# A two-block transformer on one core: the order of the first weight chunks, conv norm in pieces, pooling over band columns, residual and output in halves

## The reference, cut to what matters

```python
# block 1
mod = silu(c) @ w_ada + b_ada                      # six rows of 1024: shift, scale, gate, twice
h = rms_norm(x, norm1_w) * (1 + sc1) + sh1
proj = h @ w_in                                    # 2840 columns: q, six k/v, gates, b_gate, c_gate, u
...                                                # compressed, selected and window attention
y_conv = b_gate * short_conv(c_gate * u, conv_w)   # width 3
mix = rms_norm(concat([o_attn, y_conv]).reshape(.., 16, 64), out_norm_w)
x = x + g1 * (mix @ w_out)
x = x + g2 * hier_moe(rms_norm(x) * (1 + sc2) + sh2)      # top 2 of 64 experts
# block 2, layer l = 0, 1
h = h + g1 * (even_mixer(xn, xcn) if l == 0 else pool_mix(xn, pool_w) * pool_scale)
h = h + g2 * ((silu(hn @ w1) * (hn @ w3)) @ w2)           # 2816 hidden columns
return rms_norm(h, final_g)
```

## Time and profile before

| | before |
|---|---|
| median of three runs | 1738.36 us |
| the profiled execution | 1738.92 us, span 1737.1 us |
| TensorE matmul busy | 1390.4 us, 80% of the span |
| TensorE weight load busy | 868.6 us, 50% |
| VectorE busy | 653.3 us, 38% |
| ScalarE busy | 161.8 us, 9% |
| moved by DMA | 590.09 MB, mean 340 GB/s |
| mean granted TensorE clock | 0.901 |

### The profile page before, as it was taken

One profiled execution on the slowest core, in us unless ns is written; L12 is line 12 of the kernel. 1 busy time (PEld: TensorE's weight loads), 2 busy tenths in 40 slices (PEclk: granted clock), 3 DMA queues, 4 the chain that ended last, 5 costly groups with the idle time before them and its releaser, 6 DMA issues.

```text
span 1737.1 us, 24743 instructions
## 1 busy us (share of the span) xinstructions
PE 1390.4 (80%) x10724; PEld 868.6 (50%) x10725; DVE 653.3 (38%) x1096; ACT 161.8 (9%) x409; POOL 5.0 (0%) x10
## 2 busy tenths in 40 slices
PE   6798998766667666676667666778999999999997
PEld 4787854322212221222122112216877999989997
DVE  2367553501100110011001010107446777768775
ACT  2003320000000000000000000002422000120001
POOL 1000000000000000000000000000000000000000
PEclk9999999888888887878888898879999999999999
DMA  9989959999999999999999999996944554424541
GB/s 402 363 337 402 421 209 397 400 431 431 431 432 431 432 430 432 431 432 431 431 432 430 432 431 431 431 430 271 400 171 154 206 210 175 187 81 158 210 181 61
DMA packets 46555, 590.09 MB, mean 340 GB/s; under 512 B 5360, under 2 KB 7824, under 8 KB 9376
## 3 DMA queue, kind: packets, MB, share of 16 engines
q1 hardware_dynamic: 42896, 583.89, 80.9%
q10 hardware_dynamic: 3600, 5.34, 0.9%
HBM read 586.58 MB, written 2.62 MB: 339 GB/s over the span
## 4 chain that ended last, share of the span: by engine, by line
DMA 48%; PE 43%; DVE 6%; ACT 2%; issue 1%; SPq 0%; DVEq 0%; ACTq 0%
DMA ring<-in_w 45%; PE ps L2042 5%; PE ps L2037 4%; PE ps L2038 4%; PE ps L1551 3%; PE ps L1841 3%; PE ps L1729 3%; PE ps L1862 3%; PE ps L1488 3%; PE ps L2053 2%; PE ps L2055 2%; PE ps L2056 2%; DMA ring<-in_w_in 2%; DMA ring<-in_w_ada 1%; DVE ring_parts L819 1%; PE ps L1955 1%
## 5 line engine op out<-in xcount | busy, mean ns | idle before, releaser
L1841 PE MATMUL ps<-ring,mixT 128*32 128x512 f32 x2016 | 300.6, 732 | 161.0 <-DMA ring<-in_w 160.1
L1862 PE MATMUL ps<-ring,arena 128*32 128x512 f32 x1024 | 170.5, 799 | 112.7 <-DMA ring<-in_w 101.5
L1841 PEld LDWEIGHTS ps<-ring,mixT 128*32 128x32 f32 x2016 | 61.9, 121 | 375.1 <-issue 195.2
L1194 DVE TENSOR_TENSOR arena<-arena,ps 128x512 f32<-128x512 f32 x16 | 11.0, 689 | 488.5 <-PE ps L1841 488.5
L819 DVE TENSOR_TENSOR ring_parts<-ring,ring_parts 128x1024 fp32r<-128x1024 f32 (+3 forms) x119 | 189.7, 1625 | 1.1
L2037 PE MATMUL ps<-mixT_parts,ring_parts 128*128 128x256 f32 x704 | 169.5, 281 | 0.6 <-issue 0.6
L2038 PE MATMUL ps<-mixT_parts,ring_parts 128*128 128x256 f32 x704 | 169.4, 281 | 0.0
L1862 PEld LDWEIGHTS ps<-ring,arena 128*32 128x32 f32 x1024 | 32.7, 128 | 231.2 <-DMA ring<-in_w 150.4
L816 DVE CAST ring_parts<-ring 128x1024 fp32r<-128x1024 f32 (+3 forms) x119 | 100.4, 891 | 113.5 <-DMA ring<-in_f 72.4
L2037 PEld LDWEIGHTS ps<-mixT_parts,ring_parts 128*128 128x128 f32 x704 | 133.2, 189 | 2.1 <-issue 1.4
L2038 PEld LDWEIGHTS ps<-mixT_parts,ring_parts 128*128 128x128 f32 x704 | 132.8, 189 | 0.8
(11 more groups left out here) (379 smaller groups left out, 1421.9 us busy)
## 6 DMA issues: line engine op xcount, KB each, us to landing
ring<-in_w SPq DMA_DIRECT2D x190, 2048.0 KB, 25.8
ring<-in_ada_w SPq DMA_DIRECT2D x24, 2048.0 KB, 12.4
ring<-in_f SPq DMA_DIRECT2D x22, 2048.0 KB, 7.7
ring<-in_w_ada SPq DMA_DIRECT2D x12, 2048.0 KB, 16.4
ring<-in_f SPq DMA_DIRECT2D x22, 1024.0 KB, 5.3
ring<-in_w_in SPq DMA_DIRECT2D x5, 2048.0 KB, 22.8
ring<-in_w_out SPq DMA_DIRECT2D x2, 2048.0 KB, 11.4
ring<-in_mix_in SPq DMA_DIRECT2D x2, 2048.0 KB, 21.9
```

The lines of the kernel that those rows point to most:

```text
L1841: last = mm(ps[rows[u], j, :], XeT[:, 2 * m + k, rows[u]], w[:, u, k * FE:(k + 1) * FE], start=(m == 0 and k == 0), stop=(m == 3 and k == 1))
L1862: last = mm(ps[rows[u], m, :], heT[:, k, rows[u]], w[:, u, m * 512:(m + 1) * 512], start=(k == 0), stop=(k == FE // P - 1))
```

## The change

Seven edits, in the order of the program:

1. The numbers of the chunks. The two compression chunks, W4, W5 and W2 come earlier, and each pair of the condition chunks 6 to 11 (in the order of `w_ada`) goes behind the piece that it preceded.
2. W1 is loaded between the second and the third condition chunk, and split before the first condition round; its product takes the low part of the weights before the low part of `h`. TensorE still consumes the chunks in the order of their numbers.
3. VectorE's condition round 1 comes after the split of W5.
4. The conv's norm: ScalarE multiplies the conv result by the norm weight, four ACTIVATE of 128x256, between the square roots for q and the first `queries`; VectorE takes the reciprocal in three pieces inside attention, and one product of 128x1024 replaces the four of L992.
5. In the last step of each SwiGLU, TensorE puts the group (f = 0, t = 1, m = 1) behind (f = 1, t = 1, m = 0), and signals when t = 1, m = 0 is complete. The last two steps are written out instead of looped. `residual_ffn` takes t = 1 in two halves of 512 columns.
6. Pooling: token tile 0 gives columns 0 to 135 of the output, tile 1 columns 120 to 255, instead of all 256 each.
7. The final norm and the store run in halves of 512 columns.

```diff
--- before.py
+++ after.py
@@ -44,6 +44,7 @@
...
 CHUNK = 4096
+POOL = (2, 4, 8, 16)
 ARENA = 11264
@@ -73,9 +74,9 @@
...
 
-RA = (0, 1, 2, 3, 6, 7, 10, 11, 16, 17, 20, 21)
-RW = (24, 4, 22, 8, 14, 18)
-RC = 12
+RA = (0, 1, 2, 3, 6, 7, 14, 15, 18, 19, 22, 23)
+RW = (24, 4, 20, 8, 12, 16)
+RC = 10
 RL0 = 26
@@ -388,7 +389,7 @@
...
             front.update({RC: (A["cmp_k_w1"], CHUNK), RC + 1: (A["cmp_v_w1"], CHUNK)})
-            for n in sorted(front):
+            for n in (0, 1, RW[1], 2, 3, *sorted(n for n in front if n > RW[1])):
                 load(n, *front[n])
@@ -477,10 +478,10 @@
...
                         ffn_step(l, c, i)
-            for t in range(NT):
-                sp.wait_ge(x_new, 6 * NT + t + 1)
-                sp.dma_start(out[0, t * P:(t + 1) * P, :], xn[:, t, :]).then_inc(out_done, 16)
-            sp.wait_ge(out_done, 16 * NT)
+            for n, (t, a) in enumerate(((0, 0), (0, 512), (1, 0), (1, 512))):
+                sp.wait_ge(x_new, 6 * NT + n + 1)
+                sp.dma_start(out[0, t * P:(t + 1) * P, a:a + 512], xn[:, t, a:a + 512]).then_inc(out_done, 16)
+            sp.wait_ge(out_done, 16 * 4)
 
@@ -586,6 +587,9 @@
...
 
+            for f in range(4):
+                last = nc.scalar.activation(mixT[:, 4 + f, :], cT[:, f, :], ACT.Copy, scale=V("outn")[:, 4 + f:5 + f])
+            last.then_inc(cv_sd, 1)
             q5 = q.rearrange("p t (h i d) -> p t h i d", h=2, d=HD)
@@ -874,6 +878,7 @@
...
             norm(0)
+            split_w(RW[1], 512)
             dve.wait_ge(bias_in, 16)
@@ -881,9 +886,7 @@
...
             high_h(1, 2)
-            high_w(RW[1], 512)
             low_h(1)
-            low_w(RW[1], 512)
             split_w(RW[3], 512)
@@ -916,7 +919,6 @@
...
             split_w(RW[4], 512)
-            ada_round(1, 6)
             dve.wait_ge(tab_in, 32 + 16 * NH)
@@ -924,6 +926,7 @@
...
             split_w(RW[5], 512)
+            ada_round(1, 6)
 
@@ -970,9 +973,6 @@
...
             last.then_inc(k_n, 1)
-            dve.wait_ge(cv_sd, 1)
-            link(nc.vector.reciprocal(sq, sq))
-
             qs = xnf[:, 1024:1536].rearrange("p (h d) -> p h d", d=HD)
@@ -987,13 +987,12 @@
...
             ts(kTw, ps[:, 2, 256:512], kn[:, 2:3], None, ALU.mult).then_inc(k_ready, 1)
-            done(dve, RW[0])
-            for f in range(4):
-                last = stt(mixT[:, 4 + f, :], cT[:, f, :], V("outn")[:, 4 + f:5 + f], sq[:, f * T:(f + 1) * T], ALU.mult,
-                           ALU.mult)
-            last.then_inc(cv_mix, 1)
-            dve.wait_ge(cv_mix, 1)
+            dve.wait_ge(cv_sd, 2)
             link(nc.vector.memset(L[:, 0:2, C1 + NC:C0], 0.0))
+
+            def conv_norm(a, b):
+
+                return nc.vector.reciprocal(sq[:, a * T:b * T], sq[:, a * T:b * T])
 
@@ -1005,6 +1004,10 @@
...
                 ts(qT, ps[:, 1, 256:512], V("qn"), SCALE, ALU.mult, ALU.mult).then_inc(a_qT, 1)
+                if u == 0:
+                    conv_norm(0, 1)
+                elif u == 1:
+                    link(conv_norm(2, 4))
                 tb = tab4[:, :, u, :]
@@ -1051,8 +1054,10 @@
...
             logits(0)
+            conv_norm(1, 2)
             probabilities(0)
             logits(1)
+            tt(mixT[:, 4:8, :], mixT[:, 4:8, :], sq.rearrange("p (f t) -> p f t", f=4), ALU.mult).then_inc(cv_mix, 1)
             combined(0)
@@ -1276,6 +1281,19 @@
...
 
+            def residual_ffn(l):
+
+                dve.wait_ge(g_ev, 4 + 2 * l)
+                yy = ps[:, 4:8, :].rearrange("p (t c) n -> p t (c n)", t=NT)
+                out0, out1 = NT * (NF * (l + 1) - 1) + 1, NT * NF * (l + 1)
+                for t, cols, ready in ((0, slice(0, D), (f_out, out0)), (1, slice(0, 512), (y_first, 3 + l)),
+                                       (1, slice(512, D), (f_out, out1))):
+                    dve.wait_ge(*ready)
+                    link(tt(xn[:, t, cols], yy[:, t, cols], gB[:, cols], ALU.mult))
+                    last = tt(x[:, t, cols], x[:, t, cols], xn[:, t, cols], ALU.add)
+                    if cols.stop == D:
+                        last.then_inc(x_new, 1)
+
             def residual(b0, n, ready):
@@ -1446,7 +1464,7 @@
...
             modulation(modcol[:, 2, :], V("nmix1"))
-            residual(4, 4, lambda t: dve.wait_ge(f_out, NT * (NF - 1) + t + 1))
+            residual_ffn(0)
 
@@ -1462,13 +1480,15 @@
...
             ffn(1)
-            residual(4, 6, lambda t: dve.wait_ge(f_out, NT * (2 * NF - 1) + t + 1))
+            residual_ffn(1)
 
...
                 link(nc.vector.reciprocal(rstd[:, t:t + 1], sd2[:, t:t + 1]))
-                stt(xn[:, t, :], x[:, t, :], rstd[:, t:t + 1], rowB, ALU.mult, ALU.mult).then_inc(x_new, 1)
+                for cols in (slice(0, 512), slice(512, D)):
+                    stt(xn[:, t, cols], x[:, t, cols], rstd[:, t:t + 1], rowB[:, cols], ALU.mult, ALU.mult
+                        ).then_inc(x_new, 1)
 
@@ -1540,10 +1560,9 @@
...
 
-            def product(o, h, w, h_first, split):
-
-
-                for n, (a, b) in enumerate(((0, 0), (1, 0), (0, 1))):
+            def product(o, h, w, h_first, split, w_low_first=False):
+
+                for n, (a, b) in enumerate(((0, 0), (0, 1), (1, 0)) if w_low_first else ((0, 0), (1, 0), (0, 1))):
                     if split and n:
@@ -1578,18 +1597,17 @@
...
                                    (lambda k: hh[:, k, :], lambda k: hl[:, k, :]),
-                                   (lambda k: wH[:, k, c], lambda k: wL[:, k, c]), False, split if f == 0 else None)
+                                   (lambda k: wH[:, k, c], lambda k: wL[:, k, c]), False, split if f == 0 else None,
+                                   w_low_first)
                 return last
...
             pe.wait_ge(h_split, 1)
-            features(RW[1], 512, 2, 2, low_parts(1, 1))
+            features(RW[1], 512, 2, 2, low_parts(1, 1)[::-1], True)
             tokens(RW[1], 512, 256, [ps[:, 3, t * 256:(t + 1) * 256] for t in range(NT)], None).then_inc(ring_used, 2)
...
             features(RW[3], 512, 4, 0, low_parts(1, 2)).then_inc(ring_used, 2)
-            ada_chunk(RA[6], 6, 2, 0)
-            ada_chunk(RA[7], 6, 3, 0)
             pe.wait_ge(blk_ready, 1)
@@ -1606,9 +1624,8 @@
...
             last.then_inc(hidT_tr, 1)
-            pe.wait_ge(ada_ev, 2)
-            ada_chunk(RA[8], 6, 0, 0)
-            ada_chunk(RA[9], 6, 1, 0)
+            ada_chunk(RA[6], 6, 2, 0)
+            ada_chunk(RA[7], 6, 3, 0)
             pe.wait_ge(hidT_ev, 1)
@@ -1623,10 +1640,13 @@
...
             tr(ps[:, 7, 256:256 + NC], kcn[0:NC, :], ident[0:NC, 0:NC]).then_inc(kc_tr, 1)
+            pe.wait_ge(ada_ev, 2)
+            ada_chunk(RA[8], 6, 0, 0)
+            ada_chunk(RA[9], 6, 1, 0)
+            pe.wait_ge(win_dve, 1)
+            tokens(RW[2], 280, 0, [ps[:, 2 + t, 0:280] for t in range(NT)], low_parts(1, 5)).then_inc(ring_used, 2)
             ada_chunk(RA[10], 6, 2, 0)
             ada_chunk(RA[11], 6, 3, 0)
-            pe.wait_ge(win_dve, 1)
-            tokens(RW[2], 280, 0, [ps[:, 2 + t, 0:280] for t in range(NT)], low_parts(1, 5)).then_inc(ring_used, 2)
             pe.wait_ge(cv_sq, 1)
@@ -2043,27 +2063,39 @@
...
                 pe.wait_ge(w2_split, at(2, g + 1))
-                for f in range(2):
+
+                def down(f, t, m):
                     b = 2 * s + f
-                    pe.wait_ge(f_g, at(4, 2 * g + f + 1))
-                    for t in range(NT):
-                        for m in range(2):
-                            o = ps[:, 4 + 2 * t + m, :]
-                            tk, col = slice(t * P, (t + 1) * P), slice(m * 512, (m + 1) * 512)
-                            mm(o, r(gH[:, b, tk]), vH[:, f, col], start=(i is None and c == 0 and f == 0), stop=False,
-                               skip_group_check=True)
-                            mm(o, r(gH[:, b, tk]), vL[:, f, col], start=False, stop=False, skip_group_check=True)
-                            last = mm(o, r(gL[:, b, tk]), vH[:, f, col], start=False, stop=(c == NF - 1),
-                                      skip_group_check=True)
-                        if f == 1:
-                            last.then_inc(f_out, 1)
+                    o = ps[:, 4 + 2 * t + m, :]
+                    tk, col = slice(t * P, (t + 1) * P), slice(m * 512, (m + 1) * 512)
+                    mm(o, r(gH[:, b, tk]), vH[:, f, col], start=(c == 0 and f == 0), stop=False, skip_group_check=True)
+                    mm(o, r(gH[:, b, tk]), vL[:, f, col], start=False, stop=False, skip_group_check=True)
+                    return mm(o, r(gL[:, b, tk]), vH[:, f, col], start=False, stop=(c == NF - 1), skip_group_check=True)
+
+                pe.wait_ge(f_g, at(4, 2 * g + 1))
+                down(0, 0, 0)
+                down(0, 0, 1)
+                down(0, 1, 0)
+                if c < NF - 1:
+                    down(0, 1, 1)
+                pe.wait_ge(f_g, at(4, 2 * g + 2))
+                down(1, 0, 0)
```

(18 more changed lines are left out.)

2 lines of the change are left out of this document (1 added, 1 removed).

## The result

Over 8 runs of each, the changed kernel took 1729.53 us (1723.30 to 1734.66) and the kernel before 1738.35 us (1736.21 to 1749.82); their ratio is 0.9942, with a 95% interval from 0.9925 to 0.9959. That is 10.1 us less, between 7.1 and 13.0. The forecast was 1728.6 us, in a range from 1723 to 1737. A second set of 6 runs of the changed kernel, beside other runs of before, gave 1728.32 us and 0.9930 (0.9908 to 0.9951). The profiled execution after took 1730.26 us at a span of 1726.0, where before it was 1738.92 at 1737.1: 8.7 us less as a whole, 11.1 in the span (from the first to the last instruction). The rest lies outside it: the changed kernel spends 2.2 to 4.3 us there in its 14 runs, the kernel before 1.8 to 1.9 in all runs beside the experiments. Which edit does that is not shown (e8, e11 and e12 are back at 1.8 to 2.1).

What follows compares the result with a forecast made beforehand. Prediction: expert-weight bytes set some 900 us, TensorE is always busy behind that stream, and the front has idle time. Terms -5.9 - 3.15 + 0.14 - 0.38 - 0.5 = -9.8 us gave median 1728.6 us, range 1723 to 1737.

Steps and rivals of the forecast that it cites:

- The front, up to the first sum: From the first loads to the first attention sum: new chunk order and conv norm in pieces win 5.9 us.
- The walk: Stage-by-stage timing of the front: W1's product ends about 54, W4's 90.7, W0's low part 133.3, first attention sum 151.7 us.
- Pieces of the conv norm: Reciprocal pieces in attention hide in idle times: quarter 1.6 us in 2.13, half 3.2 in 3.25; maybe 0.2 pushed.
- the prediction's signs of being wrong: Listed failures: W4 after 80 us, VectorE holding the second sum, stream under 3 or over 9 earlier, not 4 behind it.
- Pooling: Pooling matmuls behind the first SwiGLU take 4.0 us instead of 7.17, so -3.15 us on the path.
- First SwiGLU's end: Layer 0's last step and residual: new group order and halves cost +0.14 us; writing out two steps costs nothing.
- f = 1 late: Last SwiGLU step: f = 1 is asked for one group earlier; if late, up to 0.68 us lost per layer.
- Residual of the second layer and output: End of the kernel: layer 1's residual -0.38 us, the final norm and store in halves -0.5 us.
- Front not won: Rival, 12%: loads and a slow W1 product cancel the front's gain; only -3.9 us remains, 1734.5 us.
- More won: Rival, 10%: at a high clock and without the table's reads W0 comes 3 us earlier still; 1725.5 us.
- The slower one: Rival, 5%: after the shorter pooling, the second SwiGLU begins at 1.2 GHz; with 30 us so, 1743.6 us.
- The idle DMA stretch: Between 225 and 245 us, ahead of the expert stream, DMA falls idle for about 6 us less.

Runs made afterwards that it cites:

- e8: Changed kernel with VectorE's split of the second SwiGLU's first down weights moved behind the norm after the first SwiGLU; 1727.25 us, ratio 0.9940.
- e11: Changed kernel with filler matmuls ahead of W4's and W0's products and in the first attention step, and the down-weight split behind the norm; 1723.51 us, ratio 0.9924.
- e12: Changed kernel with the last step of each SwiGLU and the residuals as in the kernel before; one run, 1727.77 us.
- e9: Kernel before with the changed front alone (new chunk order, conv norm in pieces), old pooling, residuals and output; 1731.63 us, ratio 0.9967.
- e2: Kernel before with the conv norm in pieces alone; 1735.24 us, ratio 0.9989.
- e4: Kernel before with the whole new order of the front's chunks, conv norm whole and in its old place; 1732.84 us, ratio 0.9975.
- e10: Changed kernel with filler matmuls where TensorE waits: ahead of W4's product, ahead of its low part, and ahead of W0's product; 1722.45 us, ratio 0.9920.
- e5: Changed kernel again, unaltered, beside other runs of the kernel before; 1728.32 us.
- e1: Kernel before with the pooling edit alone, 136 columns per matmul instead of 256; 1734.83 us, ratio 0.9985.
- e6: Changed kernel with filler matmuls in the front, some misplaced at W3's product and twice as long as planned; 1735.38 us, ratio 0.9983.

## Why the prediction was right, point by point

**The front, up to the first sum: right, within about half a us in the chain.** The walk said W1's product ends at 54, W4's at 90.7, W0's low part at 133.3 and the sum at 151.7; the profile has 53.86, 91.21, 133.18 and 151.98. Part of that is luck: e9 and e12 have the same front and their sums lie at 150.0 and 155.7. The medians carry the term better: 5.7 us (3.1 to 8.3) in e9 against the 5.9 forecast. That the condition chunks behind W2 pay most of W4's gain back held too: 12.2 us won at the end of W4's product, 4.7 at W0's low part.

Two errors in it cancelled. W4 landed 1.4 us before the 74.6 of the walk; the 1.5 that the walk added for the bias table, with no row for it, is not seen in this profile. And its product took 11.08 and not 9.36, since the walk took a price at the full clock and put it behind an idle time of 3.49 + 1.80 us. One inconsistency stands in the prediction: its low end for the front is 0 in the walk and 3 us won in the sum of the range; e9's interval starts at 3.1.

**Pieces of the conv norm: right up to the first sum, short behind it.** The reciprocal's pieces took 1.74, 1.74 and 3.34 us, and VectorE waited behind each in the changed kernel. But the half, forecast at 3.2 in an idle time of 3.25, took 3.34 and has no room: in e2, e9, e11 and e12 the second sum follows it within 0.1 us, without a wait for TensorE, which is one of the prediction's signs of being wrong. Its price is small, since e11's distance between the sums is 12.37 against 12.30. The larger loss (1.48 us, forecast 0) is an indirect one. Every kernel with the whole reciprocal, e4 with the new order too, has 12.3 between the sums; those with the pieces and no fitting fillers have 13.2 or more. In the kernel before, the chunk ahead of the transposes took 2.83 us, partly at the low clock, filled the wait for ScalarE's exponentials and left 1.37 us idle. With the pieces it takes 1.95 and leaves 2.97 idle, and some of the transposes behind run at 1.2 GHz: the last six took 1.54 us instead of 0.88 in the changed kernel, and all twelve were slow in e9. e11 shows the cause: fillers in that wait, the same pieces on VectorE, and 12.37. So the stream started 4.62 earlier and not 5.9. The Trainium skill, TensorE: Matmul & The Clock Gate, Part 1, says that the array is throttled unless activity releases it. By that rule, the trace agrees, with 0.90 us in e9 against 0.55 in e11 for the same three transposes.

**Pooling: right.** 3.97 us against 4.0; 3.20 won against 3.15.

**First SwiGLU's end: the step that failed.** The prediction gave +0.14 us and said that writing out two steps costs nothing. It was +1.03 and +0.60 in two profiles (12.81 and 12.38 us instead of 11.78), +0.12 in e10. VectorE's work from the landing of the next layer's first weights to the pooling is one chain, of 20.7 us before, in the changed kernel, in e5, e10 and e12; so the order and the halves by themselves cost nothing there. Before, VectorE was 0.16 us short of being the limit; the new order asks for the residual one group earlier and leaves it no slack. What moved is the landing. The load is issued 16.6 us ahead of the first down matmul in all of these, and its split begins 7.6 us behind the issue before and in e12, but 8.7 in the changed kernel, 8.2 in e5 and 7.7 in e10. These delays, 1.09, 0.63 and 0.15, match what was lost. In that stretch (from 1467 us on) the DMA view of the changed kernel has a row that before and the experiments with looped steps do not have, the one of the instruction queue (the landing is the median of two loads):

```profile
q8 instruction: 2, 0.03, 0.3%
...
ring<-in_f SPq DMA_DIRECT2D x2, 2048.0 KB, 8.7
```

All seven profiles with the two steps written out have that row (e10 with 3 packets), and their median landings are 7.8 to 8.7; the seven without have 7.6 or 7.7. That the instruction queue moves bytes there is shown; that this delays the load is not, for 0.03 MB is little, and four of the seven stand at 7.8. So the failed term is found, and the cause of the late landing stays open. The upper end of 0.68 that the prediction kept for "f = 1 late" was passed by the first profile. TensorE did wait for that half, 0.72 us, but this was not what counted: the residual began when VectorE was free, at 1501.85.

**Residual of the second layer and output: right in sum.** 1.02 us against 0.38 + 0.5. e12 splits it otherwise: 0.38 for the output, 0.64 for the residual. As the prediction had it, the residual starts 0.69 earlier relative to the last matmul, and the halves cost 0.26. The stores of 256 KB landed in 2.4 us, where those of 512 KB took 3.0: 0.6 less, as the bytes say. The fit that the Trainium skill states in DMA: Bandwidth & Descriptors, Anatomy of one DMA, is for DMAs that GpSimd issues, and not for every DMA as the prediction has it. An estimate by it is 2.6 us for 256 KB. The stores here are issued by SyncE, and the measured 2.4 stands.

**Rivals.** Front not won: refuted by e9's interval. W1's 80 matmuls took 9.36 us, so the slow W1 that it feared did not come. More won: not in the changed kernel, where W0 landed at 126.30 as in the walk; the time it named was reached only with fillers (e10, e11). The slower one, 1.2 GHz in the second SwiGLU: refuted, the clock is 1.00 there in e1 and in the changed kernel. The clock did take its toll, but in the front, behind waits of 3 to 5 us, where the prediction had it as a small part of the spread.

**The idle DMA stretch: wrong.** It was to be 6 us shorter. It is as long as before, the windows from 225 to 235 at 0.00 instead of 230 to 240: it moved with TensorE, since the six slots are full earlier too. The stream's start did follow TensorE, which is what the term needed.

**What was not forecast**: 3.55 us between the stream's start and the first SwiGLU's last step. No edit is there. Before had the chunk L1800 at 4.53 us (3.77 in the others) and 3.10 + 1.45 us in the second mixer at 1225 (1.99 + 0.87), all at the low clock. From the stream's start to the pooling the profiles spread over 5 us, so it is no gain of the change. It is why the span fell by 11.1 when what the edits did sums to 7.5. It also sets off one more sign of being wrong: behind the stream's start the span is 6.5 us shorter, and 4 were forecast. The forecast of 9.8 in all against 10.1 in the medians is thus closer than its terms were. With an interval from 7.1 to 13.0, and with losses of 1.3 in attention and 0.5 to 0.9 at the first SwiGLU's end beside the forecast, that closeness is in part luck.

## What to carry to other kernels

Cost a matmul group behind a wait at the clock that it will find there, and follow where the idle time goes when TensorE gets done sooner: here up to 1.5 us of a gain of 5.9 went into a longer wait and slower matmuls behind it. Fill such a wait with dead matmuls, but only after reading the wait's length and one filler's length from a trace: in the right place at the right length they shortened the front by 0.6 to 3.4 us, and in the wrong one at double length the kernel lost 7 (e6). And where a step is said to be hidden, write down by how much: the first SwiGLU's end had 0.16 us.

## What the runs showed of the hardware that I had not expected

- A matmul of 128x256 in f32 leaves two records of 0.226 us; the call costs 0.45. A row's "x28" for 14 calls shows it, and the mean per record alone does not.
- The same front's 2 MB load (W4) landed 73.2 to 77.2 us into the run in five profiles, with DMA share at 1.03 ahead of it in the changed kernel: near 4 us of spread, in a stage that all later ones follow. One profile can't carry a term of 2 us; 12 runs of each kernel could, with an interval of some 2 us to each side.
- Dead matmuls made a bound engine faster: 7 + 4 + 7 of them (8.4 us of TensorE's time) brought W0's product to 11.9 us in e10, where five profiles of the same front without them have 12.7 to 14.1.
